# Smaller top-k steps, gates between indexer heads, and PV behind the next keys in a one-core decoder layer

## The reference, cut to what matters

```
h = layer_norm(concat(meta, x))
qa, ka, va, ga, qi, ki, wi, cq, ckv, kpe, gb = split(h @ w_in)
# indexer: 8 heads of 64; causal
score = sum_h relu(qi_h . ki / 8) * wi_h          # meta keys: always picked
sel   = top_k(score, 128)                          # per query
# dense branch
qb = rms_norm(cq) @ w_uq;   kvb = rms_norm(ckv) @ w_ukv;  rotary part: q_pe, k_pe
pb = softmax((q_nope . k_nope + q_pe . k_pe) * scale_b)   # causal
# sparse branch
pa = softmax(qa . ka[sel] / 8 + rel_bias)
mixed = concat(pa @ va[sel] * silu(ga), pb @ vb * silu(gb))
out = layer_norm(ALPHA * h + mixed @ w_out)
```

## Time and profile before

| | us |
|---|---|
| median of 3 runs (lowest, highest) | 399.03 (398.19, 399.81) |
| the profiled execution | 399.34 |
| its span in the trace | 397.0 |
| TensorE / VectorE / ScalarE / GpSimd busy | 343.4 / 254.2 / 177.5 / 153.6 |
| first indexer head starts (L1269) | 63.62 |
| dense scores of head 0 start (L1302) | 155.27 |
| first sparse scores start (L1310) | 250.60 |

### The profile page before, as it was taken

How to read it: one execution, slowest core, us unless ns; L and a number is a source line. 1 busy time by engine, 2 the same in 40 slices (tenths; PEclk the granted TensorE clock), 3 DMA queues, 4 the chain that set the end, 5 groups by cost and what they waited for, 6 DMA issues and landing times.

```text
span 397.0 us, 6173 instructions
## 1 busy us (share of the span) xinstructions
PE 343.4 (87%) x2155; PEld 283.1 (71%) x2155; DVE 254.2 (64%) x661; ACT 177.5 (45%) x387; POOL 153.6 (39%) x138
## 2 busy tenths in 40 slices
PE   1899999999979469969989999898989959999880
PEld 0589877887858347757687869677777858987880
DVE  5742124657999992868747776566667674544784
ACT  4755554345331324253633545655476542531311
POOL 3425997413233601223352262642223230540352
PEclk9999999999998959989989999999999999999997
DMA  7282332543012412001030112330312220130112
GB/s 289 97 303 69 114 121 79 179 146 93 27 42 91 133 66 68 0 16 54 15 106 15 54 56 81 97 118 6 106 50 83 80 82 1 54 107 0 54 53 106
DMA packets 11996, 32.85 MB, mean 83 GB/s; under 512 B 2440, under 2 KB 2568, under 8 KB 11968
## 3 DMA queue, kind: packets, MB, share of 16 engines
q1 hardware_dynamic: 9376, 27.08, 20.0%
q10 hardware_dynamic: 2592, 5.40, 4.6%
HBM read 29.83 MB, written 4.81 MB: 87 GB/s over the span
## 4 chain that ended last, share of the span: by engine, by line
PE 68%; DVE 17%; issue 7%; ACT 4%; DMA 2%; ACTq 0%; SPq 0%; DVEq 0%
PE ps_j L1121 43%; PE ps_o L1363 5%; PE ps_s L1302 4%; DVE iw L984 3%; PE ps_s L1310 3%; DVE top L980 3%; PE ps_s L1269 2%; DMA res<-in_x 2%; ACT pr L762 2%; PE ps_o L1345 2%; PE ps_t L1323 1%; PE ps_s L1312 1%; ACT ks L700 1%; PE ps_t L1328 1%; PE ps_j L1166 1%
## 5 line engine op out<-in xcount | busy, mean ns | idle before, releaser
L483 POOL TENSOR_TENSOR wl<-raw,wh 128x1024 fp32r<-128x1024 f32 (+3 forms) x33 | 77.3, 2352 | 113.2 <-ACT wh L490 113.2
L1121 PE MATMUL ps_j<-hh,wh 128*128 128x512 f32 (+2 forms) x224 | 79.9, 356 | 3.5 <-POOL wl L483 3.0
L1121 PE MATMUL ps_j<-hl,wh 128*128 128x512 f32 (+2 forms) x224 | 78.5, 350 | 0.0
L1121 PE MATMUL ps_j<-hh,wl 128*128 128x512 f32 (+2 forms) x224 | 78.4, 350 | 0.0
L598 POOL TENSOR_SCALAR pr<-pr,rden 128x528 f32<-128x528 f32 (+1 forms) x64 | 34.7, 563 | 85.2 <-DVE rden L1029 85.2
L1121 PEld LDWEIGHTS ps_j<-hh,wh 128*128 128x128 f32 (+1 forms) x224 | 42.3, 189 | 10.5 <-issue 4.9
L1121 PEld LDWEIGHTS ps_j<-hl,wh 128*128 128x128 f32 (+1 forms) x224 | 42.2, 188 | 5.5 <-issue 0.2
L1121 PEld LDWEIGHTS ps_j<-hh,wl 128*128 128x128 f32 (+1 forms) x224 | 42.1, 188 | 5.6
L490 ACT ACTIVATE wh<-raw 128x1024 fp32r<-128x1024 f32 (+3 forms) x35 | 35.8, 1039 | 3.6 <-DMA raw<-in_weights 3.6
L1121 PE MATMUL ps_j<-wh,hh 128*128 128x256 f32 (+1 forms) x112 | 32.6, 291 | 2.1 <-issue 1.4
L762 ACT ACTIVATE pr<-ps_s,nm 128x528 f32<-128x528 f32 (+3 forms) x32 | 16.9, 540 | 36.8 <-DVE nm L1020 36.8
(11 more groups left out here) (211 smaller groups left out, 771.4 us busy)
## 6 DMA issues: line engine op xcount, KB each, us to landing
raw<-in_weights SPq DMA_DIRECT2D x35, 512.0 KB, 3.4
bias_by_distance<-bias_vector ACTq DMA_DIRECT2D x1, 2624.0 KB, 13.1
bias<-bias_by_distance ACTq DMA_DIRECT2D x8, 264.0 KB, 2.9
res<-in_x SPq DMA_DIRECT2D x4, 512.0 KB, 5.3
out<-res SPq DMA_DIRECT2D x6, 256.0 KB, 2.2
raw<-in_weights SPq DMA_DIRECT2D x2, 448.0 KB, 3.1
pt<-in_ln_emb_g SPq DMA_DIRECT2D x1, 512.0 KB, 5.1
pt<-in_ln_emb_b SPq DMA_DIRECT2D x1, 512.0 KB, 6.2
```

Source lines behind the costliest of these rows:

```text
L483: eng.tensor_tensor(ring_of(False, b), raw_of(b), ring_of(True, b).bitcast(F32), ALU.subtract).then_inc(done, 1)
L1121: last = pe.matmul(dst, a, b, start=n == 0 and part[0], stop=n == count - 1 and part[1])
```

## The change

The change is in the list alone, and in the semaphores that top-k needs for it.

- Top-k: each round is split in halves, half 0 the tile with 512 keys, half 1 the other three, each with its own semaphore. Three rounds stand before the rotary queries (five before), and from head 0 on a half goes between a head's maxima and its reciprocals, and another half or two behind the reciprocals. MASK goes from behind head 6 to behind the sparse keys' jobs at head 7.
- Indexer: a job stands behind each of heads 0 to 6: gate 1, query block 2, gate 2, query block 3, gates 3, 4 and 5; then gates 6 and 7 (before, gates 1 and 2 and query blocks 2 and 3 stood between heads 1 to 4), NORM 0 stands behind head 2, NORM 1 behind head 4, CAST 0 and 1 at heads 4 and 6.
- Sparse pairs: PV of a pair goes behind the jobs of the next keys; MIX 4 to 7 come one head sooner; the reciprocals of heads 14 and 15 stand behind two more output jobs, and two output jobs stand between the last two heads' transposes.

```diff
@@ -151,32 +151,37 @@
     job("gate", 0)
     order.append(("RES", 6))
     order.append(("WI",))
-    rounds = list(range(ROUNDS))
+    halves = [(r, half) for r in range(ROUNDS) for half in range(2)]
+
+    def pick(count):
+
+        for _ in range(min(count, len(halves))):
+            order.append(("TOPK", *halves.pop(0)))
 
     for h in range(HEADS):
         order.append(("I", h))
         if h in (2, 4):
-            job("gate", h // 2)
-        if h in (1, 3):
-            job("qi", h // 2 + 2)
-        if h == 1:
+            order.append(("NORM", h // 2 - 1))
+        if h < 7:
+            job(*(("gate", 1), ("qi", 2), ("gate", 2), ("qi", 3), ("gate", 3), ("gate", 4), ("gate", 5))[h])
+        if h == 0:
             order.append(("RES", 7))
-    order += [("NORM", 0), ("NORM", 1)]
-    for c in range(3, DC):
+        if h in (4, 6):
+            order.append(("CAST", h // 2 - 2))
+    order.append(("KPE",))
+    for c in range(6, DC):
         job("gate", c)
-        if c == 3:
-            order += [("CAST", 0), ("CAST", 1), ("KPE",)]
-        for _ in range((0, 1, 1, 2, 1)[c - 3]):
-            order.append(("TOPK", rounds.pop(0)))
+        pick(3)
     for g in range(2):
         job("qpe", g)
-    order.append(("TOPK", rounds.pop(0)))
+    pick(2)
     for t in range(5):
         job("uv", 0, t)
     order.append(("ZERO",))
     job("qn", 0)
     job("kn", 0, 0)
     job("kn", 0, 1)
+    pick(2)
     job("va", 0, 0)
     va = [(g, t) for g in range(2) for t in range(5)][1:]
     outs = [(g, t) for g in range(4) for t in range(QT)]
@@ -193,33 +198,39 @@
         elif more:
             jobs = [("ka", p + 1, 0), ("ka", p + 1, 1)] if g % 2 else [("qa", p + 1)]
         else:
-            jobs = [("out", *outs.pop(0)) for _ in range(6)]
+            jobs = [("out", *outs.pop(0)) for _ in range(6 if g % 2 == 0 else 4)]
+        values = [("PV", (g - 3) // 2)] if g >= 3 and g % 2 else []
         order += [("S", g), ("X", g)]
+        if g < HEADS:
+            pick(1)
         if jobs[0][0] == "qn":
             job(*jobs.pop(0), extra=0)
-        if g >= 3 and g % 2:
-            order.append(("PV", (g - 3) // 2))
-        if g == 2 * HEADS - 1:
-            job(*jobs.pop(0), extra=0)
+        if g < HEADS or not more:
+            order += values
+        if g >= HEADS and not more:
+            for _ in range(2):
+                job(*jobs.pop(0))
         order.append(("R", g))
-        if g == 0:
-            order.append(("TOPK", rounds.pop(0)))
+        if g < HEADS:
+            pick(2 if g in (4, 6) else 1)
         if g == HEADS - 1:
             order.append(("BIAS",))
         for j in jobs:
             job(*j, extra=int(j[0] == "out"))
+        if g >= HEADS and more:
+            order += values
+        if g == HEADS - 1:
+            assert not halves
+            order.append(("MASK",))
         if g:
             order += [("TP", g - 1), ("TQ", g - 1)]
         need(BLOCKS[0], 2)
-        if g < HEADS and rounds:
-            order.append(("TOPK", rounds.pop(0)))
-        if g == HEADS - 2:
-            assert not rounds
-            order.append(("MASK",))
-        if HEADS + 2 <= g < HEADS + 6:
-            order.append(("MIX", 4 + g - HEADS - 2))
+        if HEADS + 1 <= g < HEADS + 5:
+            order.append(("MIX", 4 + g - HEADS - 1))
         if g == 2 * HEADS - 2:
             order += [("MIX", 0), ("MIX", 1)]
+    for _ in range(2):
+        job("out", *outs.pop(0))
     order += [("TP", 2 * HEADS - 1), ("TQ", 2 * HEADS - 1), ("MIX", 2)]
     while outs:
         job("out", *outs.pop(0))
@@ -258,7 +269,7 @@
 MIXED = [s[1] for s in ORDER if s[0] == "MIX"]
 LAST_JOB = [NJ[last_reader(_b)] for _b in range(len(BLOCKS))]
 LAST_IN_JOB = max(n for n, j in enumerate(JOBS) if j[0] != "out")
-TOPK_OPS = 2 * QT
+TOPK_HALF = [(3,), (0, 1, 2)]
 
 
 def build(nc, x, meta, ln_emb_g, ln_emb_b, rel_bias, ln_post_g, ln_post_b, weights, gains, onehot, cos_t,
...
@@ -971,20 +982,22 @@
                                                  op0=ALU.mult, op1=ALU.add).then_inc(i_add, 1)
                 elif stage == "TOPK":
 
-                    r = arg[0]
+                    r, half = arg
+                    tiles, done = TOPK_HALF[half], topk[half]
                     if r == 0:
                         dve.wait_ge(i_add, 4 * HEADS)
-                    for i in range(QT):
+                    for n, i in enumerate(tiles):
                         if r:
-                            dve.wait_ge(topk, TOPK_OPS * (r - 1) + QT + i + 1)
-                        dve.max(top8[:, i, :], iw[:, IOFF[i]:IOFF[i] + P * (i + 1)]).then_inc(topk, 1)
-                    for i in range(QT):
+                            dve.wait_ge(done, len(tiles) * (2 * r - 1) + n + 1)
+                        dve.max(top8[:, i, :], iw[:, IOFF[i]:IOFF[i] + P * (i + 1)]).then_inc(done, 1)
+                    for n, i in enumerate(tiles):
                         a = iw[:, IOFF[i]:IOFF[i] + P * (i + 1)]
-                        dve.wait_ge(topk, TOPK_OPS * r + i + 1)
+                        dve.wait_ge(done, len(tiles) * 2 * r + n + 1)
                         dve.match_replace(out=a, in_to_replace=top8[:, i, :], in_values=a,
-                                          imm_value=TAKEN).then_inc(topk, 1)
+                                          imm_value=TAKEN).then_inc(done, 1)
                 elif stage == "MASK":
-                    dve.wait_ge(topk, TOPK_OPS * ROUNDS)
+                    for half in range(2):
+                        dve.wait_ge(topk[half], 2 * len(TOPK_HALF[half]) * ROUNDS)
                     for i in range(QT):
                         dve.tensor_scalar(mask[:, POFF[i] + META:POFF[i] + NK[i]],
                                           iw[:, IOFF[i]:IOFF[i] + P * (i + 1)], TAKEN, MASKED, ALU.is_gt,
```

More of the change, by code:

```diff
@@ L406, in build @@
         i_add = sem("i_add")
-        topk = sem("topk")
+        topk = [sem("topk_long"), sem("topk_short")]
         masked = sem("masked")
```

## The result

The changed kernel takes 415.76 us (415.01 to 417.83, four executions; a fifth on record, 413.21, isn't in the median) against 398.9 us of the kernel before in the same session: ratio 1.0415, 95% interval 1.0362 to 1.0468. It is slower, as forecast, but by 16.9 us and not by 7.5, and beyond the upper end of the range. The profiled execution took 417.83 us, 2.1 over the median; its span is 18.5 us longer than before's.

A forecast was written before the change was run, and what follows sets the result against it. TensorE, busy 343.4 of 397.0 us, was taken as the bound, its work plus its stops. The terms +10.2 + 6.8 - 5.7 + 2.6 - 6.3 = +7.6 us gave 406.5 us, with an 8-in-10 range of 399.5 to 414.

The forecast's parts named there:

- indexer stage at full clock: Indexer heads to rotary queries: 24.4 us of new weight-block stops plus 4.5 of small stops, less 18.7 removed: +10.2 us.
- its new half clock: Indexer stage: TensorE at half clock behind four of the seven new stops, 1.7 us each: +6.8, bounds 0 and 12.
- dense pairs: Dense heads: half rounds end the 4.5 us q_b wait and 1.7 of half clock, less 0.5 at k_b: -5.7 us.
- mask: First sparse scores: the mask's whole length becomes new stop, 1.6 or 3.7 us by a race with GpSimd; taken as +2.6.
- sparse pairs and output: Sparse heads and output jobs: 2.6 from PV, 3.0 from mbl and res waits, 0.7 from pt: -6.3 us.
- small stops behind: Behind the first rotary queries: old stops of 1.1, 0.5, 0.5 recur with one top-k round between: 2.1 to 5.5, taken 4.5.
- gain of PV: Sparse pairs: PV behind the next keys' jobs covers TensorE's 1.4 us waits; 1.4 at head 9, 0.6 at 11 and 13: 2.6.
- 10.9 us from the end of scores to the next scores: Sparse head 11: 5.4 to exponentials' end, 3.2 copies, 1.1 low parts, 0.7 PV product, 0.5; was 11.5, so gain 0.6.
- Rival A: Indexer stage: weights come in time, all seven stops vanish, VectorE limits the stage; about 378 us; chance 0.07.
- Rival B: The stops come but the clock doesn't fall, and the late gains are whole: 398 us, no change; chance 0.13.
- Rival C: Clock falls at all seven stops, GpSimd catches the mask, late gains are small: 415.5 us; chance 0.15.
- Rival D: Indexer: latent norm between heads delays later heads' sums on VectorE; some 2 us more; no chance of its own.

The follow-up runs named there:

- ring experiment: The changed kernel with its weight blocks taking the four slots in the order in which the jobs use them, job list unchanged: 388.08 us, ratio 0.9693.
- the two that split the change: The kernel before with only the change's indexer list: 417.44 us; the changed kernel with the old indexer list: 392.82 us.
- the mask experiment: The changed kernel with weight slots in order of use and MASK right behind head 7's last top-k half, ahead of the sparse keys: 382.84 us.
- Filling the stops: The changed kernel with ten unread matmuls ahead of each of the seven jobs that wait for weights: 405.97 us, ratio 1.014.
- the kernel with one round ahead: The changed kernel with weight slots in order of use, MASK earlier, and one top-k round instead of three ahead of the rotary queries: 377.75 us.
- the kernel with all of it: The changed kernel with weight slots in order of use, MASK earlier, late transposes of heads 8, 10, 12, one round ahead, single halves at heads 0, 1: 370.56 us.

## Why the prediction was right in sign and wrong in size

By its own steps, in the profiled executions (span +18.5 us), with half clock counted as half of the busy time, as the prediction does:

| term | forecast | measured |
|---|---|---|
| indexer stage at full clock | +10.2 | +8.8 |
| its new half clock | +6.8 | +12.6 at the seven stops, +1.7 behind q_b |
| dense pairs | -5.7 | -7.1 |
| mask | +2.6 | +3.6, and 1.8 of clock |
| sparse pairs and output | -6.3 | about -3.0 |
| sum | +7.6 | +18.4 |

**Right.** Seven stops for weight blocks, in the places named: 23.2 us for 24.4. Their lengths came from durations in the earlier trace rows: making a block less one head. Those behind gates were 2.83 for 3.0, behind query jobs 3.44 for 3.6. The ring experiment shows the cause, and the two that split the change show that this list alone costs +17 to +23 us. The small stops behind were 4.3 for 4.5. The 7.6 on VectorE and the 4.5 for q_b went (0.4 in its place, so 4.1); among the dense pairs both half-clock stretches are gone, 3.4, of which the forecast had counted one. The stretch itself gives the -7.1 of the table: 88.23 us with the mask out of the way (the mask experiment), 95.33 before. The reciprocals, the low half of the mixed rows and pt brought 4.35 in the output stage for 3.7.

**The step that failed** is the clock: "Bounds 0 and 7 x 1.7 = 12; I take four of seven, 6.8." Measured by the same count were 12.6 at the seven stops, a little over its own upper bound, and 1.7 behind the wait for q_b, for which the sum had no clock: 14.3. Two things were off in it. Six of seven stops had half clock behind them, so the middle was no fair reading of "every stop of 2.9 us or more in this trace (three of them)"; and the bound counted one stretch of 3.41 a stop, though the earlier trace rows has a stretch of 10.24 with 6.74 of busy TensorE, worth 3.4 us. Two of the new stretches lasted 6.83. Filling the stops gave 9.8 us back, so this term is shown, and with 14.3 in the place of 6.8 the forecast would have been 414. The price per stretch, 1.7, was a little high besides (3.41 us at 45% are 1.5).

**Mis-sized besides.** The mask was a race as forecast, and its upper end came, 3.6 for 3.7, but by another instruction: not a conversion, the add. The Trainium skill, page "SBUF — State Buffer", section "SBUF: two separate sides", has whichever comes later blocked for the whole instruction of the other. The add agrees: it took 2.33 us beside blocks of 2.33, behind the start of the first by 0.11, and 0.23 alone. What the prediction worked out by that rule, one of the two ends and not the middle, came true, while the sum had taken the middle. The half clock at a stop that had grown from 1.4 to 5.0 was not priced: 1.8. The gain of PV, 2.6, was 0.3 of stops, and the 1.8 us stop before 339.68 had half clock behind it, 1.7. The step that failed there is "10.9 us from the end of scores to the next scores". In after head 11's scores end at 305.56 (their last mask product, 305.22 and 0.34) and these rows follow on ScalarE, VectorE and TensorE:

```profile
311.57 3.23 ACT L711 ACTIVATE ks<-ps_j 64x264 fp32r<-64x264 f32 x8
...
316.14 0.69 DVE L1060 TENSOR_TENSOR mix<-ps_o,mix 128x512 f32<-128x512 f32 x1
...
316.89 0.55 PE L1358 MATMUL ps_o<-ident,pr 128*128 128x128 f32 x3 [1.76 <-DVE mix L1060]
317.19 0.47 PE L1323 MATMUL ps_s<-ks,qs 128*128 128x240 f32 x2
```

The exponentials end where the key copies begin, 6.0 behind the scores and not 5.4 as at the earlier trace rows; the low parts end 1.3 behind the copies and not 1.1; the next scores start 11.6 behind the last ones' end, where before had 11.5. In before PV was in the chain: ScalarE's second half of the key copies waited for the key job behind it.

```profile
293.26 1.61 ACT L700 ACTIVATE ks<-ps_j 64x264 fp32r<-64x264 f32 x4 [1.30 <-PE ps_j L1121]
```

In after PV lies beside the chain: the copies run in one piece behind the exponentials, and the product behind PV stands at its end. One chain went and another as long came. Moving the waiting transposes behind the scores took that product out of the chain, and brought 5.2.

**Rival A** (weights in time, 378) had the mechanism of the ring experiment and was 10 us too low for it: the stops vanish, but VectorE's 8.8 and the mask's 5.0 stay. Rival B is refuted by the windows above. Rival C had the time, 415.5, and most of the mechanism; its 0.15 was too little. In part its hit is luck: the clock fell at six stops and not at seven, and twice for longer. Rival D didn't come: no wait for the norm or the sums shows in the ring kernel.

Open: why the stop that ended at 125.68 kept the clock, when those of equal length at 114.24 and 135.58 didn't. The stops alone don't settle it: the kernel with one round ahead and the kernel with all of it have the same list up to the rotary queries and the same two stops there (1.67 and 1.76 us), but the profile of the first has half clock for 3.4 us at the second stop and that of the other 1.00; and executions of one kernel differ in their mean granted clock. In the sparse pairs stop and clock rows add up to some 0.9 us more than the stretch grew.

## What to carry to other kernels

When work is moved in a list that several in-order queues share, move the order of the buffers' reuse with it: here one line of the ring's order was worth 27.7 us, and turned the change from 4% slower to 3% faster. Price a stop of TensorE near 3 us as the stop and the half clock behind it, and take the bound of the clock from the longest stretch seen, not from the commonest. A clock that falls in one execution of a kernel can stay up in the next, so a single trace prices this term only roughly. A wait that is taken from one instruction turns up at the next one in the same queue that needs the late result, unless that one is moved too.

## What the hardware showed that was not expected

- Half clock at the end of a 3.44 us and of a 2.83 us stop lasted 6.83 us, and 3.4 at others of 2.83 to 4.11; one of 2.83 had none.
- At a granted clock of 0.50 products of 512 columns started 0.427 us apart, at 1.00 every 0.233: the half clock took 45% of the busy time, not half.
- The same list with the same stops of 1.67 and 1.76 us had half clock at the second in one profile and none in another.
- Unread matmuls in the stops held the clock at 1.00 up to the dense values and saved 9.8 us, though 7.2 us of stops, the longest 1.8 there and 2.9 at the rotary queries, were left.
- A VectorE add of 144 columns took 2.33 us beside a GpSimd block that had started 0.11 us before it, and 0.23 us alone.
